# Hybrid decoder step on one core: stacked 16-bit products for the sample states, and a new order of the work in the head groups

## The reference

```
s_new = exp(b_last)[..., None] * s0 + einsum('bshk,bshv->bhkv', k * exp(b_last[:, None] - b), v)   # HGRN2
s_new = exp(c * log_gamma) * s0 + einsum('bshk,bshv->bhkv', k * k_dec, v)                           # retention
```

## Time and profile before

| what | value |
| --- | --- |
| median of 3 runs | 1737.02 us (1736.96 to 1738.49) |
| profiled execution, its time | 1742.57 us |
| profiled execution, its span | 1741.0 us |
| mean granted PE clock | 0.931 of full |
| PE busy | 1567.8 us (90%) |
| DVE, ACT, POOL busy | 904.5, 654.0, 154.3 us |

### The profile page before, as it was taken

The page is one execution under the profiler, slowest core; times in us unless marked ns, Lnnn a source line. Parts: engine busy times, 40 slices in busy tenths (PEclk is TensorE's granted clock), DMA queues, the critical chain, the costliest instruction groups (busy, mean ns, idle before and its releaser), DMA issues.

```text
span 1741.0 us, 31399 instructions
## 1 busy us (share of the span) xinstructions
PE 1567.8 (90%) x12107; PEld 1251.0 (72%) x12107; DVE 904.5 (52%) x1389; ACT 654.0 (38%) x920; POOL 154.3 (9%) x126
## 2 busy tenths in 40 slices
PE   4699999989699999999867999999886999999994
PEld 3477777767578888788755777777765888887883
DVE  4766644444565555533266665444356555553334
ACT  3645523332353334422155452333225443333213
POOL 2111111100200000000030111000002000000002
PEclk8799989988899999999978899999888999999997
DMA  6132222221123332233221224232031223322321
GB/s 192 46 90 77 75 75 75 74 74 55 57 73 97 96 96 77 70 93 95 82 66 51 74 74 111 57 88 78 27 97 48 88 83 96 96 81 74 97 66 51
DMA packets 175035, 138.05 MB, mean 79 GB/s; under 512 B 5064, under 2 KB 169192, under 8 KB 174776
## 3 DMA queue, kind: packets, MB, share of 16 engines
q1 hardware_dynamic: 168192, 113.46, 22.0%
q0 software_dynamic: 5408, 18.60, 3.8%
q10 hardware_dynamic: 1372, 5.16, 0.9%
HBM read 125.12 MB, written 12.07 MB: 79 GB/s over the span
## 4 chain that ended last, share of the span: by engine, by line
PE 77%; DVE 9%; ACT 6%; issue 4%; DVEq 2%; ACTq 1%; DMA 1%; SPq 0%
PE ACC L510 61%; PE SCR L624 2%; PE OT L632 2%; PE SCR L662 1%; ACT WH L830 1%; DVE X L1193 1%; PE OT L684 1%; PE SCR L545 1%; PE SCR L727 1%; DVE Z L1222 1%; DVE Fb L1206 1%; DVE WL L1153 1%; PE OT L600 1%; DVEq L1261 1%; PE OT L599 1%
## 5 line engine op out<-in xcount | busy, mean ns | idle before, releaser
L510 PE MATMUL ACC<-XH,WH 128*128 128x280 f16 x2432 | 502.6, 289 | 70.8 <-DVE XL L1196 43.1
L510 PE MATMUL ACC<-XL,WH 128*128 128x280 f16 x2432 | 502.4, 289 | 0.0
L510 PE MATMUL ACC<-XH,WL 128*128 128x280 f16 x2432 | 501.6, 289 | 0.0
L510 PEld LDWEIGHTS ACC<-XH,WH 128*128 128x128 f16 x2432 | 238.7, 101 | 153.0 <-DVE XL L1196 45.6
L1153 DVE SCALAR_TENSOR_TENSOR WL<-stage,WH 128x2048 f16<-128x2048 f32 (+1 forms) x116 | 245.9, 2120 | 182.0 <-ACT WH L830 170.2
L510 PEld LDWEIGHTS ACC<-XL,WH 128*128 128x128 f16 x2432 | 243.3, 100 | 58.6
L510 PEld LDWEIGHTS ACC<-XH,WL 128*128 128x128 f16 x2432 | 243.3, 100 | 58.0
L830 ACT ACTIVATE WH<-stage 128x2048 f16<-128x2048 f32 (+1 forms) x116 | 204.8, 1766 | 103.7 <-PE ACC L510 86.9
L510 PE MATMUL ACC<-shared,WH 128*128 128x280 f16 x1408 | 225.2, 283 | 0.2
L510 PEld LDWEIGHTS ACC<-shared,WH 128*128 128x128 f16 x1408 | 137.6, 98 | 30.8 <-issue 0.8
L510 PE MATMUL ACC<-shared,WL 128*128 128x280 f16 x704 | 141.5, 283 | 0.0
(11 more groups left out here) (238 smaller groups left out, 1791.4 us busy)
## 6 DMA issues: line engine op xcount, KB each, us to landing
stage<-in_w_in_dram SPq DMA_DIRECT2D x64, 512.0 KB, 5.3
stage<-in_w_a_dram SPq DMA_DIRECT2D x44, 512.0 KB, 4.3
stage<-in_w_b_dram SPq DMA_DIRECT2D x44, 512.0 KB, 4.8
stage<-in_w_down_dram SPq DMA_DIRECT2D x32, 384.0 KB, 3.3
stage<-in_w_down_dram SPq DMA_DIRECT2D x32, 320.0 KB, 3.7
out_dram<-shared POOLq DMA_DIRECT2D x16, 512.0 KB, 3.9
stage<-in_w_o_dram SPq DMA_DIRECT2D x16, 512.0 KB, 3.9
shared<-in_state_hgrn_dram POOLq DMA_DIRECT2D x8, 512.0 KB, 5.7
```

The source lines that it names most:

```text
L510: last = mm(ACC[:, acc, h, 0:HALF], lhs, x[:, xk + k, h * HALF:(h + 1) * HALF], start=begin, stop=end)
```

## The change

Keys and values of the sample tokens are stacked three times along the partitions (96 rows), as 16-bit numbers: high keys with high values, high keys with low values, low keys with high values. One 16-bit matmul of 96 rows then gives what a float32 matmul of 32 rows gave. For this KE and V get two more copies of the 32 sample columns (DVE and ACT), the transposes take 96 columns, ACT copies the result twice (KV3 in 16 bits, KVF in float32), and DVE makes the low parts (`low_sample_rows`), which POOL now waits for (`kv_low`). Besides that the order changes: DVE does the chunk states ahead of `hg_exponents`, ACT reads the query ahead of `hg_exponentials` in all HGRN groups, ACT's retention copies go ahead of weight split 1, and ahead of the output projection the retention stage goes ahead of the gate on ACT and DVE. The slots stay.

```diff
 T = TP + TS
+TS3 = 3 * TS
 HALF = T // 2
...
     put("mask32", causal)
-    put("seq", tok[:, None] // DEC_SEQ == np.arange(DEC_BATCH)[None, :])
+    put("seq", np.tile(tok[:, None] // DEC_SEQ == np.arange(DEC_BATCH)[None, :], (3, 1)))
     log_g = np.log1p(-np.exp2(-5.0 - np.arange(HEADS)))
...
     put("k_dec", np.where(left >= 0, np.exp(np.maximum(left, 0) * log_g[None, None, :]), 0.0) * root)
-    put("k_dec_s", np.exp((DEC_SEQ - 1 - tok % DEC_SEQ)[:, None] * log_g[None, :]) * root)
+    put("k_dec_s", np.tile(np.exp((DEC_SEQ - 1 - tok % DEC_SEQ)[:, None] * log_g[None, :]) * root, (3, 1)))
     put("gamma4", np.broadcast_to(np.exp(DEC_SEQ * log_g), (P, HEADS)))
...
         Fb, T1, T2, T3, B, Q, QS, QD, KE, E, V, G = (
-            sb(n, [P, T + 2]) for n in ("Fb", "T1", "T2", "T3", "B", "Q", "QS", "QD", "KE", "E", "V", "G"))
+            sb(n, [P, T + (2 * TS if n in ("KE", "V") else 2)]) for n in ("Fb", "T1", "T2", "T3", "B", "Q", "QS", "QD", "KE", "E", "V", "G"))
         at = [0]
...
         AX, CX = (T1, T2), (T3, Fb)
-        VX = sb("VX", [TS, DEC_BATCH, P])
-        KVTS = sb("KVTS", [TS, 2, P])
+        VX = sb("VX", [TS3, DEC_BATCH, P], F16)
+        KV3 = sb("KV3", [TS3, 2, P], F16)
+        KVF = sb("KVF", [TS3, 2, P])
         PTS = sb("PTS", [C, TP])
...
         tok_ready, vx_ready, pts_ready, states_ready = sem("tok_ready"), sem("vx_ready"), sem("pts_ready"), sem("states_ready")
+        kv_low = sem("kv_low")
         decays_used = sem("decays_used")
...
             return ap.unsqueeze(2).to_broadcast([ap.shape[0], ap.shape[1], n])
+
+        def twice(t):
+
+            return t[:, T:T + 2 * TS].rearrange("p (a t) -> p a t", a=2)
...
-                pool.wait_ge(tok_ready, hh + 1)
-                nc.gpsimd.tensor_tensor(VX[:, :, :], KVTS[:, 1:2, :].to_broadcast([TS, DEC_BATCH, P]), bcast(seqm[0:TS, :], P),
+                pool.wait_ge(kv_low, hh + 1)
+                nc.gpsimd.tensor_tensor(VX[:, :, :], KV3[:, 1:2, :].to_broadcast([TS3, DEC_BATCH, P]), bcast(seqm[0:TS3, :], P),
                                         ALU.mult).then_inc(vx_ready, 1)
...
                         for i, src in enumerate(sources):
-                            last = nc.tensor.transpose(SCR[0:TS, bank, i * P:(i + 1) * P], src[:, TP:T], ident)
+                            last = nc.tensor.transpose(SCR[0:TS3, bank, i * P:(i + 1) * P], src[:, TP:TP + TS3], ident)
                     last.then_inc(scr_full, 1)
...
                 job(scr, bank)
-                mm(SCR[:, bank, :], KVTS[:, 0, :], VX[:, 4 * n:4 * n + 4, :].rearrange("p b v -> p (b v)"),
+                mm(SCR[:, bank, :], KV3[:, 0, :], VX[:, 4 * n:4 * n + 4, :].rearrange("p b v -> p (b v)"),
                    start=True, stop=True).then_inc(scr_full, 1)
...
                 cols_ = OT[:, 1, TP - SPLIT:REST]
-                mm(cols_, KVTS[:, 1, :], PTSS[:, :], start=True, stop=False, skip_group_check=True)
+                mm(cols_, KVF[0:TS, 1, :], PTSS[:, :], start=True, stop=False, skip_group_check=True)
                 for b in range(DEC_BATCH):
...
                         nc.tensor.transpose(SCR[0:TAIL, 0, n * P:(n + 1) * P], src[:, 4 * P:TP], ident)
-                        last = nc.tensor.transpose(SCR[0:TS, 0, (2 + n) * P:(3 + n) * P], src[:, TP:T], ident)
+                        last = nc.tensor.transpose(SCR[0:TS3, 0, (2 + n) * P:(3 + n) * P], src[:, TP:TP + TS3], ident)
                     last.then_inc(scr_full, 1)
...
                 act.wait_ge(acc_full, 1 + tile + 1)
-                f(halves(buf[:, 0:T]), ACC[:, c, :, 0:HALF], ACT.Copy, scale=INV_W).then_inc(acc_read[c], 1)
+                last = f(halves(buf[:, 0:T]), ACC[:, c, :, 0:HALF], ACT.Copy, scale=INV_W)
+                if buf is V:
+                    last = f(twice(V), ACC[:, c, 1:2, HALF - TS:HALF].to_broadcast([P, 2, TS]), ACT.Copy, scale=INV_W)
+                last.then_inc(acc_read[c], 1)
                 if done is not None:
...
                 act.wait_ge(scr_full, full)
-                f(KVTS[:, :, :], SCR[0:TS, 0, 0:2 * P].rearrange("p (n v) -> p n v", n=2), ACT.Copy).then_inc(scr_read[0], 1)
+                f(KV3[:, :, :], SCR[0:TS3, 0, 0:2 * P].rearrange("p (n v) -> p n v", n=2), ACT.Copy)
+                f(KVF[:, :, :], SCR[0:TS3, 0, 0:2 * P].rearrange("p (n v) -> p n v", n=2), ACT.Copy).then_inc(scr_read[0], 1)
                 act.drain().then_inc(tok_ready, 1)
...
                 f(VTOK[0:TAIL, 4 * P:5 * P], SCR[0:TAIL, 0, P:2 * P], ACT.Copy)
-                f(KVTS[:, 0, :], SCR[0:TS, 0, 2 * P:3 * P], ACT.Copy, scale=tab[0:TS, ds(cols["k_dec_s"][0] + p, 1)])
-                f(KVTS[:, 1, :], SCR[0:TS, 0, 3 * P:4 * P], ACT.Copy).then_inc(scr_read[0], 1)
+                for rows_ in (KV3, KVF):
+                    f(rows_[:, 0, :], SCR[0:TS3, 0, 2 * P:3 * P], ACT.Copy, scale=tab[0:TS3, ds(cols["k_dec_s"][0] + p, 1)])
+                    last = f(rows_[:, 1, :], SCR[0:TS3, 0, 3 * P:4 * P], ACT.Copy)
+                last.then_inc(scr_read[0], 1)
                 act.drain().then_inc(tok_ready, 1)
...
                 hh = l * 2 * HEADS + kind * HEADS + head
+                if b is not None:
+                    a()
                 split_hi(1, j, (acc_full, 1 + tile))
...
                     out_gate(hh - 1)
-                if a is not None:
+                if a is not None and b is None:
                     a()
...
                 if kind == 0:
-                    if d is None:
-                        read_acc(Q, 1, tile + 1, None)
+                    read_acc(Q, 1, tile + 1, None)
                     hg_exponentials(l, head)
-                    if d is not None:
-                        read_acc(Q, 1, tile + 1, None)
                 split_hi(0, j + 1, (acc_full, 1 + tile + 2))
...
                     group(l, p + HEADS + 1, p + 1, 1, rt_stages(l, p))
+                a, b, _, c, d = rt_stages(l, HEADS - 1)
+                a()
                 out_gate((l + 1) * 2 * HEADS - 1)
-                for stage_ in rt_stages(l, HEADS - 1):
-                    if stage_ is not None:
-                        stage_()
+                b()
+                c()
+                d()
...
-            def hg_gate(l, p, tile):
+            def low_sample_rows(hh):
+
+                dve.wait_ge(tok_ready, hh + 1)
+                for n, rows_ in enumerate((slice(2 * TS, TS3), slice(TS, 2 * TS))):
+                    tt(KV3[rows_, n, :], KVF[rows_, n, :], KV3[rows_, n, :], ALU.subtract)
+                dve.drain().then_inc(kv_low, 1)
+
+            def hg_gate(l, p, tile, low_rows=None):
                 n = l * HEADS + p
...
                 dve.drain().then_inc(f_ready, 1)
+                if low_rows is not None:
+                    low_rows()
...
                 tt(QD[:, 0:T], Q[:, 0:T], E[:, 0:T], ALU.mult)
+                nc.vector.tensor_copy(twice(KE), KE[:, TP:T].unsqueeze(1).to_broadcast([P, 2, TS]))
                 dve.drain().then_inc(ew_ready, 1)
...
                 tt(QS[:, TP:T], QD[:, TP:T], tab[:, ds(cols["q_dec"][0] + p * TS, TS)], ALU.mult)
+                nc.vector.tensor_copy(twice(KE), KE[:, TP:T].unsqueeze(1).to_broadcast([P, 2, TS]))
                 dve.drain().then_inc(ew_ready, 1)
...
                 dve.drain().then_inc(pts_ready, 1)
+                low_sample_rows(hh)
...
                 split_lo(1, j)
+                hgrn_rows = (lambda: low_sample_rows(hh - 1)) if steps else None
                 if kind == 0:
-                    hg_gate(l, head, tile)
-                    hg_exponents(l, head)
+                    hg_gate(l, head, tile, hgrn_rows)
                     if b is not None:
                         b()
+                    hg_exponents(l, head)
                     if d is not None:
...
+                        hgrn_rows()
                         dve.wait_ge(tok_ready, hh)
...
                     group(l, p + HEADS + 1, p + 1, 1, rt_stages(l, p), ot0 + 2 + HEADS + 2 * p)
+                a, *others = rt_stages(l, HEADS - 1)
+                a()
                 out_gate((l + 1) * 2 * HEADS - 1)
-                for stage_ in rt_stages(l, HEADS - 1):
+                for stage_ in others:
                     stage_()
...
                 zero_sums()
```

## The result

The changed kernel takes 1725.09 us (median of 4 runs, 1724.96 to 1726.71) against 1737.76 for the kernel before: ratio 0.9927, 95% interval 0.9913 to 0.9941. It is 12.7 us faster, where 25 were forecast. The direction and the range hold, the size does not.

A forecast was written before the change was run, and what follows sets the result against it. PE, busy 90%, was taken as the bound, with DVE and ACT's loop next in HGRN groups. Per layer -12.5 us, twice -25, from the profiled 1742.6 gave 1717.6; the median lying 5.5 lower, 1712, range 1696 to 1733.

The forecast's parts named there:

- What bounds the kernel: Whole kernel: PE bounds it, busy 90% of the span; its waits and L624's product make some 71 us.
- The second loop: HGRN groups: the loop through DVE and ACT, hidden by 2.1 us before, grows to 40.3 us and holds PE.
- the wait at L609: HGRN groups, slot 28: PE waits about 5 us for DVE's sample additions L1300, with half clock behind it.
- The loop's terms: HGRN group: 16.2 + 20.3 + 3.8 = 40.3 us, plus 2.2 for half clock: 42.5, 1.3 slower.
- By that L1206 runs between VX and L423 and ends 1.2 us earlier than now: HGRN groups: DVE's L1206 gets in between POOL's two instructions and ends 16.2 us into the group.
- The second rival: POOL keeps the port: L423 goes first, L1206 ends 1.85 us later in 8 groups; 1727 us; chance 0.25.
- The pair of 2.69 us: Layer norm: two POOL instructions take 2.69 us alone, 3.68 with DVE at work, so DVE gets in between.
- group 1: First HGRN group forecast: change of 0, since its longer starting stretch at half clock falls away.
- The stacked product: Sample product on PE: 0.22 us per 16-bit matmul; 1.6 us saved per HGRN group, 1.5 per retention group.
- the three new waits: Retention groups: added waits of 0.4 (second ACT copies), 0.25 (POOL's VX) and 0.15 us (DVE's query).
- The retention order: Groups 6 and 7 lose the 1.86 us wait at L653; last head gains 2.9 us plus 2.4 of half clock.
- third rival: POOL's spread VX (96 rows, 16-bit output) becomes the bound: 1730 us at 3.0 us, 1746 at 4.0; chance 0.08.

The follow-up runs named there:

- e7: Changed kernel with a drain of POOL between the value spread and the decay; 1727.6 us, ratio 0.9930.
- e13: Changed kernel with POOL's decay first and spread second, at the same place behind the low parts; 1731.9 us, ratio 0.9959.
- e11: Changed kernel, chunk states back behind the exponents, POOL's decay moved into DVE's idle gap (groups 1 to 3; after pts_ready in group 4); 1693.4 us.
- e2: Changed kernel with POOL's decay of the sample states ahead of the value spread, as soon as the old states are in; 1725.4 us, ratio 0.9931.
- e5: Changed kernel with all three orders put back, leaving only the stacked 16-bit product, its copies and low parts; 1729.8 us, ratio 0.9949.
- e1: Changed kernel with DVE's chunk states put back behind the exponents, the query read staying early; 1715.0 us, ratio 0.9880.
- e4: Kernel before with only the retention order changed on ACT and DVE; 1718.2 us, ratio 0.9887.
- e14: Kernel before with the retention order and POOL's decay in DVE's idle stretch, float32 products, query read behind the exponentials; 1689.6 us, ratio 0.9713.
- e8: Changed kernel with DVE's sample additions ahead of the key product, while DVE waits for ACT's exponentials; 1710.0 us, ratio 0.9820.

## Why the prediction was wrong

*What bounds the kernel* held. The second loop, hidden by 2.1 us before, is the bound of the HGRN groups after, with the wait at L609 where it was said to be and of the size said (5.86 us against "about 5").

*The loop's terms*, forecast against measured in group 2:

| stretch | forecast | measured |
| --- | --- | --- |
| group's start to the gate addition's end | 16.2 | 150.34 - 132.04 = 18.3 |
| from there to the additions' end | 20.3 | 170.82 - 150.34 = 20.5 |
| mean of squares to the group's end | 3.8 + 2.2 | 176.5 - 170.87 = 5.6 |
| sum | 42.5 | 44.4 |

**The step that failed** is "By that L1206 runs between VX and L423 and ends 1.2 us earlier than now". It was taken from the layer norm. POOL went straight on to the decay and the gate addition ended 0.9 us later than before instead of 1.2 earlier, 2.1 us in each group. The second rival had this case (44.4 us a group), and its 1727 is near the measured 1725.1. That is in part luck: it also made group 4 1.85 us longer than forecast, and group 4 came out 0.9 shorter.

But the step was wrong more deeply than in who goes first: e7 and e13 show that even when the gate addition does get in, a DVE instruction close behind it waits for the second POOL instruction, and the group takes 44.4 us all the same. From the gate addition's start to the scan's it is 4.10 us in the changed kernel, 3.77 in e7 and 4.12 in e13, but 2.38 in e11, where the decay is out of the way. So 1.4 to 1.7 us should have been charged to DVE's chain in either order. e2 gives the same size: with the decay done long before, the mean of squares begins 1.9 us earlier.

The layer norm was also read too simply. The pair of 2.69 us was not alone; DVE worked beside it:

```profile
877.37 0.99 DVE L1184 TENSOR_TENSOR T<-SCR,T 128x280 f32<-128x280 f32 x2 [3.78 <-ACTq L844]
878.46 1.29 DVE L1188 TENSOR_SCALAR T<-T 128x560 f32<-128x560 f32 x1
```

L1184 reads PSUM (SCR), and beside it POOL's two instructions took no longer than the shortest of that line (1.35 us each); so it is with the chunk states in e7's group 4. L1188 ended only behind the pair (879.45) and took 1.29 us, where L1209 of the same size takes 0.45: this is the case of the clamp in e7, and the trace of before had it.

The failed step makes about 2 us in each of four groups (2 and 3 of both layers), and together with group 1 (which was given 0 and cost 1.3 in all, by two rows that do not agree) 9 us of the missing 12. The median gives the rest: in the profiled executions the change is 15.8 us, since the one of before lay 4.8 us above its median and the one of after 1.6.

*The stacked product* was priced rightly on PE: from the second L631 at 155.75 to the next L517 at 155.97 is 0.22 us. What was wrong is how much of it PE could use. For retention groups the three new waits were forecast at 0.8 us and are 0.2 (copies) and 0.5 (spread) in group 6; that fits. Group 5 has 0.4 and 0.5 and gained 0.2 us where 0.7 was forecast; the rest was not traced. For the last head 0.8 (spread) and 0.4 (copies) were forecast, and 1.1 and 0.8 were measured. For the HGRN groups no credit was taken, rightly. Summed over the kernel it gives 8 to 10 us alone (e5). On top of the retention order, together with the early query read, it gives 3 (e1 against e4, whose intervals overlap), and none in the best order (e11 against e14). The query read was never moved by itself.

*The retention order* was sized well. In e4, where it stands alone, groups 6 and 7 lose 5.2 us and the output projection 4.7 in layer 1; the forecast's terms for it, without those of the products, are 5.5 and 5.3. Alone it gives 19 us, three quarters of all that was forecast. So the change's 12.7 us are about 19 from this, 3 from the stack and the query read, and about 10 lost to the moved chunk states (e1 against the changed kernel).

What stays open: why the output projection takes between 91.6 and 100.1 us in these kernels. Between the changed kernel and e11 its DVE and ACT work is the same, and its mean granted clock differs: 0.88 in the changed kernel, 0.81 in e11, 0.85 in e14. The stretch of the changed kernel, then that of e11 (columns as in the earlier trace rows):

```profile
379.50:472.80 93.30, 72.52 (x518) 56.98 (x515) 50.75 (x62) 31.84 (x48) 15.45 (x12) 0.88 0.19 58
```

```profile
358.90:455.60 96.70, 76.38 (x518) 59.45 (x515) 50.70 (x62) 31.83 (x48) 15.36 (x12) 0.81 0.18 56
```

The same instructions run (518 records of PE), 3.4 us apart. What sets the clock there was not tried. The difference is as large as the differences between the best four kernels, so these are not ranked.

## What to carry to other kernels

A wait that is removed by doing its work earlier is paid by all that stands behind that work on its engine. Before moving it, add up that engine's chain to the next thing PE needs, and compare with how much PE will have gained: here 2.1 us of slack against 5.5 us of gain. Look instead for idle time (e8 put the additions into 2.5 us in which DVE was idle, e11 POOL's decay into 2 us of the same) and leave the chain alone.

Work taken from the busiest engine counts only where that engine is not waiting within the same group. Price the helper work (copies, low parts, the wait of POOL for them) against it: here, in the best order, it left nothing of a product that became nearly five times shorter.

## What the runs showed of the hardware

Two POOL instructions back to back kept a ready DVE instruction out until both were done (L1229, 2.84 us), though by the records it started 0.33 us before the second. The Trainium skill, "SBUF — State Buffer", section "Who interferes with whom", has issue order decide; by that L1229 would have gone first, and the measurement is against it. With a drain between them (e7) or the two swapped (e13) it did go first. In these cases who goes first could not have been forecast. Who pays depends on what DVE does next: in groups 2 and 3 it was the clamp (e7, 2.00 us) or the subtraction L1229 (e13, 2.43 us), in group 4 of e7 the chunk states, which read PSUM, and they did not wait at all.

The tensor_scalar of e7, with one SBUF input, was blocked as well: 2.00 us instead of 0.45. The same section names tensor_scalar among those that can take the shared pair, and this trace agrees.

POOL's spread takes 1888 ns with 96 rows and 16-bit output and 1886 with 32 rows and float32, so the change of rows and types together left its time as it was. The forecast's third rival is out by this.
